# Two layers of retention and neighbourhood attention on one core: attention in steps of both heads of a pair, and four products at once on the array's column groups

## The reference, cut to what matters

```python
sh1, sc1, g1, sh2, sc2, g2 = adaln(c, w_ada[l], b_ada[l])       # silu(c) @ w_ada + b_ada
hm = modulate(rmsnorm(x, norm_pre_mix[l]), sh1, sc1)
rq, rk, rv, rg, nq, nk, nv = project_in(hm, w_in[l])
y, _, _ = retention_bidir(rq, rk * k_scale, rv, log_g, s0_f, s0_b)
# neighbourhood attention: 8 heads of 64 features; a window of 8 x 16 keys with a bias, and 128 cached keys
p = softmax(concat([q @ k_window + bias, q @ k_ctx]))
y_na = p[window] @ v_window + p[ctx] @ v_ctx
x = block_tail(x, hm, y_ret, y_na, ...)                         # gates, w_o, norms, SwiGLU
```

## Time and profile before

| | |
|---|---|
| median of 3 runs | 2354.46 us (2350.59 to 2357.75) |
| the profiled execution | 2355.82 us, span 2354.0 us |
| busy | PE 2267.7 us (96%), DVE 1283.7 (55%), ACT 841.1 (36%) |
| first step of attention, layer 0 and layer 1 | 458.89 and 1604.68 us |
| mean granted clock of TensorE | 0.987 of full speed |

### The profile page before, as it was taken

The page is one execution under the profiler, slowest core; times in us unless marked ns, Lnnn a source line. Parts: engine busy times, 40 slices in busy tenths (PEclk is TensorE's granted clock), DMA queues, the critical chain, the costliest instruction groups (busy, mean ns, idle before and its releaser), DMA issues.

```text
span 2354.0 us, 33977 instructions
## 1 busy us (share of the span) xinstructions
PE 2267.7 (96%) x14512; PEld 2131.6 (91%) x14512; DVE 1283.7 (55%) x1979; ACT 841.1 (36%) x1327; POOL 86.8 (4%) x160
## 2 busy tenths in 40 slices
PE   7999988999989999999979999999999999999997
PEld 3999988999978999999969999999999799999996
DVE  3555577466746867667475555225655533343434
ACT  4555332355335221221265444224543431222212
POOL 0000010000000000000000000000000000000000
PEclk9999999999999999999999999999999999999999
DMA  6212155221533543433412121232223222222121
GB/s 244 86 64 69 62 176 164 100 73 62 180 90 137 173 137 128 150 117 126 108 44 86 63 63 60 81 96 82 71 93 126 72 90 81 72 69 84 54 90 45
DMA packets 59750, 233.62 MB, mean 99 GB/s; under 512 B 7312, under 2 KB 7344, under 8 KB 57424
## 3 DMA queue, kind: packets, MB, share of 16 engines
q1 hardware_dynamic: 41040, 153.12, 20.0%
q0 software_dynamic: 18560, 78.33, 9.7%
HBM read 223.00 MB, written 8.42 MB: 98 GB/s over the span
## 4 chain that ended last, share of the span: by engine, by line
PE 86%; DVE 6%; ACT 3%; issue 2%; DMA 2%; DVEq 0%; ACTq 0%; SPq 0%; POOL 0%; POOLq 0%
PE unit L402 16%; PE unit L403 16%; PE unit L405 16%; PE unit L390 11%; PE unit L392 10%; PE unit L391 10%; DVE junk L1372 2%; PE sc L390 1%; DMA raw<-w_main 1%; PE unit L483 1%; PE sc L392 1%; PE sc L391 1%; DVE wl L1272 1%; DVE ptl L1282 1%; PE tp L654 1%
## 5 line engine op out<-in xcount | busy, mean ns | idle before, releaser
L402 PE MATMUL unit<-hmh,wh 128*128 128x320 f32 x2304 | 694.1, 309 | 1.2 <-issue 0.8
L403 PE MATMUL unit<-hml,wh 128*128 128x320 f32 x2304 | 694.0, 309 | 0.0
L1272 DVE TENSOR_TENSOR wl<-raw,wh 128x1024 fp32r<-128x1024 f32 x276 | 335.4, 1223 | 360.4 <-ACT wh L937 353.8
L405 PE MATMUL unit<-hmh,wl 128*128 128x320 f32 x2304 | 525.0, 309 | 0.0
L402 PEld LDWEIGHTS unit<-hmh,wh 128*128 128x128 f32 x2304 | 432.5, 188 | 3.3 <-issue 1.9
L403 PEld LDWEIGHTS unit<-hml,wh 128*128 128x128 f32 x2304 | 432.6, 188 | 1.5
L405 PEld LDWEIGHTS unit<-hmh,wl 128*128 128x128 f32 x2304 | 385.2, 188 | 0.0
L937 ACT ACTIVATE wh<-raw 128x1024 fp32r<-128x1024 f32 x276 | 283.8, 1049 | 120.4 <-DMA raw<-w_main 120.4
L1372 DVE CUSTOM_DVE_ANT_0 junk<-ada,csb,par 128x1024 f32<-128x1024 f32 x160 | 205.6, 1285 | 23.7 <-DMA ada<-w_ada 4.0
L390 PE MATMUL unit<-wh,hmh 128*128 128x256 f32 (+1 forms) x640 | 201.1, 314 | 12.1 <-DVE hml L1282 5.1
L392 PE MATMUL unit<-wh,hml 128*128 128x256 f32 (+1 forms) x640 | 199.3, 311 | 0.0
(11 more groups left out here) (282 smaller groups left out, 3476.0 us busy)
## 6 DMA issues: line engine op xcount, KB each, us to landing
raw<-w_main SPq DMA_DIRECT2D x276, 512.0 KB, 3.7
ada<-w_ada POOLq DMA_DIRECT2D x80, 512.0 KB, 3.9
bias<-biases POOLq DMA_DIRECT2D x16, 640.0 KB, 5.0
first<-w_first SPq DMA_DIRECT2D x8, 1024.0 KB, 21.0
x<-x POOLq DMA_DIRECT2D x2, 2560.0 KB, 12.1
gains<-g_rows POOLq DMA_DIRECT2D x4, 1024.0 KB, 5.2
x_keep<-x POOLq DMA_DIRECT2D x1, 2560.0 KB, 10.2
x<-x_keep POOLq DMA_DIRECT2D x1, 2560.0 KB, 9.6
```

The lines of the kernel that those rows point to most:

```text
L402: pe.matmul(u[:, h, 0:n], a[0], xs[h][0], start=f, stop=False)
L403: pe.matmul(u[:, h, 0:n], a[0], xs[h][1], start=False, stop=False)
L405: mm = pe.matmul(u[:, h, 0:n], a[1], xs[h][0], start=False, stop=z)
L1272: dve.tensor_tensor(wl[slot[i]][:, :], raw[slot[i]][:, :], f32(wh[slot[i]][:, :]), ALU.subtract)\
```

## The change

1. **Attention by pairs.** A step is now both heads of a pair at one block: 20 steps for a layer instead of 40. `score` issues the same matmuls, alternating between the head in partitions 0 to 63 (into `sc[0]`) and the one in 64 to 127 (into `sc[1]`). `turn` for both heads follows at once, then all pieces of the step, then `weigh` for both heads. DVE does the two reductions, the low part of the first head's transposed step, both normalisations, the other low part. The probabilities of the second head get buffers of their own (`pth1`, `ptl1`), laid over slots 2 and 3 of the weights' ring. So slabs 46 to 55 use slots 0 and 1 alone, and slots 4 to 7 come in at slab 56. By the rule for the slots, slab 46 takes the slot of 44 and 47 that of 45 in layer 0, and those of 42 and 43 in layer 1, where the ring stands two further on. The two `split`s behind the first step are gone; seven are spread over the steps, one comes behind the low parts of the result, and one place after it takes two for one.
2. **Bias in three parts a head**, loaded and negated part by part; the sums over the two halves of a value product in two parts.
3. **Shift and scale.** The four products of a slab write partitions 0, 32, 64 and 96 of one bank instead of four banks' partitions 0 and 1; ACT and DVE copy two rows each. DVE takes half of the copies of the transposed x.
4. **Decays** move on DVE and ACT from the start to behind the first split slabs.

```diff
-WIDE, W_O, LAST = 58, 64, 130
+NARROW, WIDE, W_O, LAST = 46, 56, 64, 130
...
-STEPS = NPAIR * 10
+STEPS = NPAIR * 5
...
+        pth = [n1("pth", [P, 2, 2, NS], F32R), at("pth1", [P, 2, 2, NS], wl_at + (RING + 2) * SLAB * 4, F32R)]
+        ptl = [n1("ptl", [P, 2, 2, NS], F32R), at("ptl1", [P, 2, 2, NS], wl_at + 2 * SLAB * 4, F32R)]
...
-            may = range(RING) if j < WIDE or LAST <= j < LAST + 4 else range(RING, RING + MORE) if j >= LAST - 2 else range(RING + MORE)
+            may = range(2) if NARROW <= j < WIDE else range(RING) if j < WIDE or LAST <= j < LAST + 4 else range(RING, RING + MORE) if j >= LAST - 2 else range(RING + MORE)
...
+        SPLIT_AT = (3, 6, 8, 11, 13, 16, 20)
...
-                    mm = pe.matmul(unit[n // 2][0:2, n % 2, :], cc[:, k, :], wf[k][:, n * 512:(n + 1) * 512],
+                    mm = pe.matmul(unit[0][32 * n:32 * n + 2, 0, :], cc[:, k, :], wf[k][:, n * 512:(n + 1) * 512],
...
+                        for t, (a, b) in enumerate(terms):
+                            for hh in range(2):
+                                pe.matmul(sc[hh][:, 0:n], (nqh, nql)[a][rows[hh], j * P:(j + 1) * P],
+                                          (nkh, nkl)[b][rows[hh], first * P:first * P + n], start=t == 0, stop=t == 2)
+                        for t, (a, b) in enumerate(terms):
+                            for hh in range(2):
+                                mm = pe.matmul(sc[hh][:, n:n + P], (nqh, nql)[a][rows[hh], j * P:(j + 1) * P],
+                                               (ckh, ckl)[b][rows[hh], p, :], start=t == 0, stop=t == 2)
...
             act.wait_ge(const_set, 1)
-            act.wait_ge(lg_z, 1)
-            act.activation(lt[:, 0, :], lt[:, 1, :], ACT.Exp, scale=-1.0).then_inc(lg_e, 1)
             act.wait_ge(x_back, 16)
...
             split(2)
+            act.wait_ge(lg_z, 1)
+            act.activation(lt[:, 0, :], lt[:, 1, :], ACT.Exp, scale=-1.0).then_inc(lg_e, 1)
             act.wait_ge(const_in, CONSTS)
...
-            dve.wait_ge(early_in, EARLY)
-            decays()
             for t in range(TILES):
                 scaled(t)
...
             split(2)
+            decays()
             dve.wait_ge(const_in, CONSTS)
...
-                    if g == 0:
-                        split(2)
```

More of the change, by code:

```diff
@@ L341, in build @@
         STREAMS = ((0, slice(0, NS)), (1, slice(NS, T)))
+        BIAS_AT = [slice(KIND_AT[n], KIND_AT[n] + KIND_W[n] + P) for n in range(3)]
         EARLY, CONSTS = 16 * 4, 16 * 3
@@ L624, in half_columns, with score @@
                                 yield
[L626 to L632, removed]
+                def score(i):
+                    p, j = divmod(i, 5)
+                    pe.wait_ge(s_ready, (l * STEPS + i) * 2)
+                    if p >= 1 and j < 2:
+                        pe.wait_ge(lin_free[j], l * 8 + 2 * p)
                     nqh, nql, nkh, nkl = nqk[p % 2]
-                    rows = slice(64 * hh, 64 * hh + 64)
+                    rows = [slice(64 * hh, 64 * hh + 64) for hh in range(2)]
+                    terms = ((0, 0), (0, 1), (1, 0))
                     if j < 4:
@@ new lines, in score @@
+                        for t, (a, b) in enumerate(terms):
+                            for hh in range(2):
+                                mm = pe.matmul(sc[hh][:, n:n + P], (nqh, nql)[a][rows[hh], j * P:(j + 1) * P],
+                                               (ckh, ckl)[b][rows[hh], p, :], start=t == 0, stop=t == 2)
+                    else:
+                        for t, (a, b) in enumerate(terms):
+                            for hh in range(2):
+                                mm = pe.matmul(sc[hh][:, 0:P], (nqh, nql)[a][rows[hh], NS:T], (nkh, nkl)[b][rows[hh], NS:T],
+                                               start=t == 0, stop=t == 2)
@@ L667, in weigh @@
                     if group == 2:
-                        parts = [(vals(4), av[:, 1, 0:P], pch[:, :], pcl[:, :])]
+                        parts = [(vals(4), to, pch[hh][:, :], pcl[hh][:, :])]
                     else:
                         odd = (1, 0)[group]
[L671 to L674, removed]
@@ L681, in weigh @@
+                        for n in range(2):
+                            at_ = slice((n + 1) * P, (n + 2) * P)
+                            parts.append((vals(group * 2 + n), to, pth[hh][:, group, :, at_], ptl[hh][:, group, :, at_]))
+                    for n, (val, out, hi, lo) in enumerate(parts):
+                        pe.matmul(out, val, hi, start=n == 0, stop=False)
+                        mm = pe.matmul(out, val, lo, start=False, stop=n == len(parts) - 1)
                     mm.then_inc(pt_done, 1)
@@ new lines, in _ @@
+                for i in range(STEPS + 3):
+                    p, j = divmod(i, 5)
+                    if 1 <= i <= STEPS:
+                        turned_high(i - 1, 0)
+                    if i < STEPS:
+                        n = width(j)
+                        for hh in range(2):
+                            v = j * 2 + hh
+                            act.wait_ge(s_ready, (l * STEPS + i) * 2 + hh + 1)
+                            act.activation(s[:, hh, 0:n], s[:, hh, 0:n], ACT.Exp, bias=nmax[:, v:v + 1], scale=-1.0,
+                                           accum_out=sums[:, v:v + 1]).then_inc(e_ready, 1)
+                    if 1 <= i <= STEPS:
+                        turned_high(i - 1, 1)
+                    if i < 2:
+                        negative_biases(0, i + 1)
+                    for q, h in halves_at(i):
+                        half_column(q, h)
+                    for q, half in sums_at(i):
+                        of, cols = AV_HALF[half]
+                        for hh in range(2):
+                            there, here = (slice(64 * (n % 2), 64 * (n % 2) + 64) for n in (hh, hh + 1))
+                            act.wait_ge(pt_done, (l * NPAIR + q) * 6 + (1, 5)[half] + hh)
+                            if q == 0 and half == 0:
+                                act.wait_ge(nv_saved, (l + 1) * 16)
+                            act.activation(avs[there, cols], av[here, hh, of], ACT.Copy).then_inc(av_half, 1)
+                    if i in SPLIT_AT:
+                        split()
+                    if j == 2 and p < NPAIR - 1:
+                        negative_biases(p + 1, 0)
+                    if j == 4 and p < NPAIR - 1:
+                        negative_biases(p + 1, 1)
+                    if j == 1 and 0 < p < NPAIR:
+                        negative_biases(p, 2)
```

287 lines of the change are left out of this document (143 added, 144 removed).

## The result

The changed kernel takes 2312.74 us (median of 4 runs, 2310.76 to 2314.79) beside 2355.57 for the kernel before (4 runs, 2350.59 to 2357.75). The ratio is 0.9813, 95% interval 0.98 to 0.9826.

What follows compares the result with a forecast made beforehand. PE was taken to bound the kernel, with 86% of the chain of waits. The terms summed as 2355.8 - 27 - 8 + 12.5 + 2.4 + 0.8 - 1.2 = 2335.3 us profiled, 2334 in the runs; range 2317 to 2350.

Steps and rivals of the forecast that it cites:

- score products overlap: Attention: score products of a pair's two heads overlap on the row halves, 27 us less; ends 12 and 33.
- transposes, pieces, value products: Attention: they stay as many; the sum had no term for them.
- waits in the stages, clock in layer 1: Attention: of 11 us of PE waits and low clock, 8 us are gained; ends nothing and all.
- entry of layer 0: Before layer 0's first score PE waits for slots of slabs 44 and 45: 12.5 us more; ends 9 and 15.
- clock behind it: After the wait at layer 0's attention entry, PE's clock is low for 4.8 us: 2.4 us more.
- slab 55: At the attention stage's end this slab lands late; PE may wait some 0.8 us over both layers.
- start: Modulation 7.9 us earlier, but moved decays delay PE: net 1.2 us less; ends 3.5 less and 6.8 more.
- Rows without overlap: Rival, attention score: row halves do not overlap, 12 us instead of 27 saved, 2349 us; chance 0.13.
- column groups without overlap: Rival, start: the four products of a shift-and-scale slab do not run at once, 2342 us; chance 0.05.
- an entry without a wait: Rival, layer 0's attention entry: slots fall otherwise than counted, no wait, 2319 us; chance 0.08.
- Alternating costs: Rival, attention score: each change of row half drains the array, 2414 us at 0.15 a change; chance 0.07 with other losses.
- DVE as the bound: Rival, attention: every step a serial chain, DVE bounds the pairs, 10 us over eight pairs, 2344 us; chance 0.11.

Runs made afterwards that it cites:

- transposes apart: Changed kernel with the second head's transposes moved behind half of the step's pieces, apart from the first head's: 2309.83 us, ratio 0.9799.
- heads apart: Changed kernel with the first head's transposes of the step before put between the two heads' score products: 2346.14 us, ratio 0.9959.
- column groups alone: Kernel before with the new start's four products on column groups and divided copies, decays left in front, attention untouched: 2347.63 us, ratio 0.9967.
- ring turned: Changed kernel with the first four slabs in slots 2, 3, 0, 1, so slab 46 follows 42 in layer 0 too: 2298.48 us, ratio 0.9754.
- heads in turn: Changed kernel with three score products of the first head issued before the same three of the second: 2310.57 us, ratio 0.9806.
- whole heads: Changed kernel with all six score products of head 0 issued before all six of head 1: 2323.47 us, ratio 0.9866.
- decays in front: Changed kernel with the decays back at the start, ahead of the scaling of x and the roots: 2306.30 us, ratio 0.979.

## Why the prediction was right in direction and too small

The account by the steps of the prediction, forecast and measured on the spans:

| term | forecast | measured | from |
|---|---|---|---|
| score products overlap | -27 | -33.3 | steps of 0.84, 1.00, 0.48 for both heads: 4.16 less a pair, x 8 |
| transposes, pieces, value products | 0 | -11.3 | what is left of PE's busy time in the two stages |
| waits in the stages, clock in layer 1 | -8 | -10.4 | idle 11.6 to 2.85, and 1.6 of clock |
| entry of layer 0 | +12.5 | +12.1 | wait in the timeline |
| clock behind it | +2.4 | +2.4 | 4.9 us at 0.50 |
| slab 55 | +0.8 | 0 | no row of such a wait |
| start | -1.2 | -1.8 | end of the values |
| elsewhere | 0 | -2.7 | 1.4 and 1.3 behind the stages |
| sum | -20.5 | -45.0 | |

The second row is worked out so: PE's busy time fell by 20.0 + 23.8 = 43.8 us; 2.4 of low clock were added in layer 0 and 1.6 taken away in layer 1 (129.81 against 128.23 for the same 866 matmuls), so 44.6 at one clock, less 33.3.

**The step that failed, first.** "Transposes, pieces and value products stay as many": their number did, their time did not, and the sum had no term for it, nor had its best end; with it the range would have reached the result. (The best end as it stands, 2317, also drops the 2.4 us of clock although it keeps 9 us of waiting; every run here with a wait at this entry has the lower clock behind it.) Summed from the timelines of the ordinary pair, by the distance from each start to the next: 96 products of the pieces took 15.1 us before and 14.7 after, the 36 value products 5.2 (the wait of 0.9 taken off) and 4.4, the 30 transposes 3.2 both times. The layers' stages give 1.4 a pair, more than the middle pair's 1.2; what makes up the rest was not traced.

Nearly all of the 1.2 us lies at the two edges of a score, where products of 64 rows meet products of 128. In the kernel before:

```profile
501.37 0.60 PE L654 MATMUL tp<-ident,s 128*128 128x128 f32 x4
501.90 0.38 PE L390 MATMUL sc<-nkh,nqh 64*128 64x256 f32 x1
...
502.73 0.41 PE L390 MATMUL unit<-hmh,wh 128*128 128x320 f32 x1
502.98 0.31 PE L391 MATMUL unit<-hml,wh 128*128 128x320 f32 x1
```

The last transpose stands 0.20 us before the score, where transposes stand 0.11 apart, and the first product behind the score 0.25 before the next, where others stand 0.147. With a piece or a value product in front of the score the loss is the same 0.09. There were ten such scores a pair, about 2.1 us of edges, and there are five now, with a transpose behind each at 0.17 instead of 0.11, about 0.8. The timelines book most of this on pieces and value products, because these were the neighbours. Where transposes meet the other full-height products nothing is lost.

Two runs bear this out. The one with the transposes apart doubles the edges of the transposes alone and costs nothing. The one with the heads apart doubles the edges of the scores and costs 0.75 us a pair beyond the second head's products. So 0.75 of the 1.2 is shown by a run. The rest, for edges with pieces and value products in place of transposes, is argued from the distances.

**The step that failed, second.** The mechanism was right and the size off: "two products of 128 columns need 0.12 together". They need 0.06, since the rows show the second head's start at the same time as the first's, in every form. The term was 27 and measured 33.3, the full overlap that I had as its end. I took the middle because weights are loaded for every matmul and thought the loads of two halves would queue. No row of before spoke for that; the two ends were rows, the middle was a guess. The Trainium skill (TensorE: Matmul & The Clock Gate, "Part 3: Packing small matmuls") gives 3.07 times for four row tiles; for two row halves this trace shows 2.0 times, 0.84 us for 12 products as for 6.

**The waits** were the right ones, but both the reading and the share were too small. The forecast had 11 us, of which 9.5 idle; the stages had 11.6 us idle and 1.6 of clock, 13.2 in all, because the last pair of a layer waited 2.4 us and not the 1.35 that the 9.5 holds for it. It took 8 of its 11, and 10.4 of 13.2 came. DVE never became the bound, as the pair without idle time shows. Of the 2.85 us that are left 2.5 stand in a stage's last pair, as assumed. The 1.6 of clock are no sure gain: in the run with the column groups alone, where the attention is that of the kernel before, the stages lasted 137.2 and 136.4 us at a clock of 0.98 and 0.97 instead of 134.1 and 135.6.

**The entry** came out as it was worked out, to 0.4 us in the wait and to the tenth in the clock, from the slot's number and the row of today's second slab; the run with the ring turned confirms both (14.5 forecast, 14.3 measured). Without it the changed kernel would have been faster by 0.6% more.

**The start** came out as well: modulation at 41.48 (forecast 41.0), PE standing for 6.5 (6.7), resumed at 66.40 (66.7), clock 0.52 behind it.

**The rivals.** Rows without overlap, column groups without overlap and an entry without a wait are excluded by rows. "Alternating costs" is excluded twice: 12 alternating products take the time of six, and alternated and in turn take the same. DVE as the bound is excluded by the pair in which PE has no idle time. The rule that I set beside it (the Trainium skill, TensorEngine Tiling (Array Packing), "Key Properties": a change of mode drains, a change of tile does not) agrees with this case: 12 products on alternating halves cost as 6 on one.

**What stays open.** 2.7 us went in stages that the change does not touch, 1.4 between the attention stages and 1.3 behind the second. The windows of these two stretches, of the kernel before, of the changed kernel, and of the run with the heads apart; last the first stretch in the run with the heads in turn:

```profile
592.97:1604.68 1011.71, 986.63 (x6352) 941.05 (x6352) 595.40 (x818) 347.04 (x508) 46.45 (x81) 0.99 0.34 108
1740.26:2354.00 613.74, 593.57 (x3532) 554.65 (x3532) 260.54 (x275) 162.99 (x227) 4.26 (x8) 0.99 0.25 82
```

```profile
578.81:1589.09 1010.28, 986.67 (x6352) 940.73 (x6352) 597.77 (x821) 347.79 (x511) 48.02 (x84) 0.99 0.34 109
1696.56:2309.00 612.44, 594.97 (x3532) 555.70 (x3532) 263.03 (x278) 164.96 (x230) 4.27 (x8) 0.99 0.25 84
```

```profile
597.08:1604.69 1007.61, 986.46 (x6353) 940.86 (x6353) 598.08 (x821) 347.84 (x511) 48.20 (x84) 0.99 0.34 109
1729.79:2339.20 609.41, 591.94 (x3532) 553.07 (x3532) 263.11 (x278) 165.09 (x230) 4.29 (x8) 0.99 0.25 84
```

```profile
577.28:1592.31 1015.03, 992.83 (x6353) 946.72 (x6353) 597.94 (x821) 347.80 (x511) 48.01 (x84) 0.99 0.34 109
```

With the heads in turn, where the attention takes the changed kernel's time, the first stretch is 4.7 us longer, and PE is 6.2 us longer busy with the same matmuls. With the heads apart the second stretch is 3.0 us shorter, all of it in PE's busy time for the same 3532 matmuls. So, with one execution of each traced, these stretches differ by several us between kernels that are the same there, and the 2.7 lie within that. Why the clock and the waits differ was not traced. That three products, and not a time or another resource, are the limit in the run with whole heads rests on one form of step at two widths.

## What to carry to other kernels

Two products of 64 rows on different row halves, each into a bank of its own, cost as one here (12 in 0.84 us as six before), whether the heads alternate or come three products at a time; look for heads, halves or tiles that can be put beside each other, and keep every full-height instruction out from between them. When a ring of slots is narrowed, write down which slab takes whose slot at the entry of the stage, in every layer: one list of start values was worth 14 us here. Count the edges between products of half and of full height: each of the five scores a pair that fell away gave about 0.2 us here, while a group of transposes among other full-height products cost nothing. And work that is moved out of idle time into a busy engine's queue must be checked against the next instruction behind it: the decays took back 6.4 of 8 us.

When a cost has two ends that rows give and a middle that is only reasoned, the range has to hold both ends, and the sum of the best ends must include the neighbours of what changes.

## What the runs showed of the hardware

Matmuls on different row halves start out of program order. The seventh of twelve started before the fourth, and with the first when it was the fourth. The Trainium skill (TensorE: Matmul & The Clock Gate, "Part 3: Packing small matmuls") says that matmuls start and end strictly in order; the rows at 497.50 and 497.61 of the run with whole heads say otherwise for starts, and the measurement decides. How far ahead was three unstarted products, no more, and the price of passing it was 0.35 us in a step of 0.84. Whether the two heads also need banks of their own was not tried; the column groups overlapped in one bank, and transposes of all 128 rows into different tiles did not overlap (0.109 us each).

TensorE's clock fell to the 1.2 GHz level after PE had stood 6.5 and 12.1 us, and the five us of work behind each were granted 0.52 and 0.50. After shorter waits it went either way. In the kernel before it was 0.51 behind 3.1 us. Before PE's `values` of the first head it was 1.00 behind 2.79 us in the run with the decays in front and behind 2.32 in the kernel before, but 0.66 behind 1.91 in the run with the column groups alone. So these runs give no length of wait up to which the clock stays, and a gain that counts on it is not a sure one.
